# Seven sets of expert weights, down weights on GpSimd's queue, and eight value pages outside the ring

## The reference

```python
h = rmsnorm(x); z = h @ w_in                      # nine parts, 1024 -> 8192
ret = retention_output(retention(q_r, k_r, v_r, state_ret), g)      # 4 heads, decayed states
att = moba_attend(rope(q_a), keys, values)        # 8 sample rows read 8 pages each of cache_k, cache_v
y   = x + (gate_r * (ret @ w_ret_o) + gate_a * (att @ w_att_o)) @ w_o
h2  = rmsnorm(y)
group = top1(h2 @ w_router); two = top2 inside the group (8 experts each, 4 groups)
y  += sum over the two experts of  g_e * (silu(h2 @ w_gate[e]) * (h2 @ w_up[e])) @ w_down[e]
out = rmsnorm(y) * norm_final
```

## Time and profile before

| | us |
|---|---|
| median of 3 runs | 768.91 (768.21 to 770.3) |
| profiled execution | 769.54 |
| its span | 767.7 |
| TensorE busy | 653.7 (85%) |
| VectorE, ScalarE, GpSimd busy | 308.1, 141.3, 139.2 |
| read from HBM, written | 235.00 MB, 9.11 MB |

### The profile page before, as it was taken

How to read it: one execution, slowest core, us unless ns; L and a number is a source line. 1 busy time by engine, 2 the same in 40 slices (tenths; PEclk the granted TensorE clock), 3 DMA queues, 4 the chain that set the end, 5 groups by cost and what they waited for, 6 DMA issues and landing times.

```text
span 767.7 us, 13776 instructions
## 1 busy us (share of the span) xinstructions
PE 653.7 (85%) x5037; PEld 459.7 (60%) x5037; DVE 308.1 (40%) x1554; ACT 141.3 (18%) x404; POOL 139.2 (18%) x209
## 2 busy tenths in 40 slices
PE   6999999999899987989998999827996848767593
PEld 4888887787788765744433877626654525443341
DVE  3005988998867775610000221444324201111114
ACT  3222223223235222210010000121110101000012
POOL 0169954761000223200000000011000000000000
PEclk9999999999999999999999999958998969787898
DMA  9939899789978999579999989457699999999971
GB/s 306 273 110 321 284 305 393 263 280 354 360 252 269 338 322 350 171 276 402 399 410 383 291 330 381 174 225 266 245 392 401 388 387 401 402 403 399 415 283 58
DMA packets 93830, 243.00 MB, mean 317 GB/s; under 512 B 8786, under 2 KB 54482, under 8 KB 85442
## 3 DMA queue, kind: packets, MB, share of 16 engines
q1 hardware_dynamic: 56818, 192.99, 67.1%
q10 hardware_dynamic: 31328, 32.00, 12.8%
q0 software_dynamic: 5616, 17.11, 6.5%
HBM read 235.00 MB, written 9.11 MB: 318 GB/s over the span
## 4 chain that ended last, share of the span: by engine, by line
PE 55%; DMA 26%; DVE 14%; issue 2%; SPq 1%; ACT 1%; POOL 0%; DVEq 0%; ACTq 0%; POOLq 0%
PE zps L885 31%; DVE kall L1367 7%; DMA qb<-in_w_down 6%; DMA hT<-in_w_down 6%; PE zps L1202 4%; PE nps L1179 4%; PE nps L1054 4%; DMA ring_all<-in_w_ret_o 4%; DMA ring_all<-in_w_down 3%; DMA out<-sfin 2%; PE nps L856 2%; DMA kall<-in_cache_k 2%; DMA gain<-v_rows 2%; PE zps L856 1%; PE bps L1217 1%
## 5 line engine op out<-in xcount | busy, mean ns | idle before, releaser
L885 PE MATMUL zps<-hT,ring_all 128*128 128x264 f32 x1152 | 276.3, 394 | 1.6 <-DVE hT L1548 1.0
L885 PEld LDWEIGHTS zps<-hT,ring_all 128*128 128x128 f32 x1152 | 218.3, 194 | 45.6 <-issue 5.6
L1367 DVE CUSTOM_DVE_ANT_0 kall<-kall,qb 128x128 f32<-128x128 f32 x512 | 153.2, 366 | 59.8 <-DMA kall<-in_cache_k 57.1
L596 POOL DMA_INDIRECT zatt<-h_rows,tidx_i x16 | 15.1, 943 | 361.3 <-DVEq L1636 199.8
L1054 PE MATMUL nps<-ring_all,zret 128*64 128x512 f32 x256 | 59.1, 600 | 5.4 <-DMA ring_all<-in_cache_v 4.3
L885 PE MATMUL zps<-headT,ring_all 128*128 128x264 f32 x256 | 58.5, 388 | 4.9 <-DMA ring_all<-in_w_ret_o 3.5
L885 PEld LDWEIGHTS zps<-headT,ring_all 128*128 128x128 f32 x256 | 48.2, 190 | 16.0 <-issue 6.0
L1709 DVE TENSOR_TENSOR qdT<-qdT,nps 128x64 f32<-128x64 f32 x32 | 7.1, 221 | 118.6 <-ACT qdT L801 118.1
L645 ACT ACTIVATE zt<-zps 128x264 f32<-128x264 f32 x56 | 21.8, 390 | 153.6 <-PE zps L885 147.5
L1535 DVE TENSOR_TENSOR hT<-zps,zatt 128x264 f32<-128x264 f32 x8 | 3.5, 433 | 96.4 <-PE zps L885 96.3
L1367 DVE DVE_READ_ACCUMULATOR2_ANT scores<- 128x1 f32 x512 | 40.9, 80 | 0.0
(11 more groups left out here) (360 smaller groups left out, 829.1 us busy)
## 6 DMA issues: line engine op xcount, KB each, us to landing
kall<-in_cache_k SPq DMA_DIRECT2D x64, 512.0 KB, 6.5
ring_all<-in_cache_v SPq DMA_DIRECT2D x64, 512.0 KB, 8.1
ring_all<-in_w_in ACTq DMA_DIRECT2D x26, 1024.0 KB, 8.4
ring_all<-in_w_gate SPq DMA_DIRECT2D x12, 1024.0 KB, 18.8
ring_all<-in_w_up SPq DMA_DIRECT2D x12, 1024.0 KB, 21.8
ring_all<-in_w_down SPq DMA_DIRECT2D x12, 1024.0 KB, 14.5
ring_all<-in_w_in SPq DMA_DIRECT2D x6, 1024.0 KB, 13.5
kall<-in_w_gate SPq DMA_DIRECT2D x5, 1024.0 KB, 22.6
```

The costliest lines, as they stand in the source:

```text
L596: pool.indirect_dma_start(out=rows, out_offset=None, in_=h2_rows, in_offset=bass.IndirectOffsetOnAxis(ap=col, axis=0), bounds_check=T - 1, ...
L885: mm = pe.matmul(zps[m % 2][:, 0:T], w[:, k, P * fb:P * (fb + 1)], rhs[:, k, :], start=(k == 0), stop=(k == KT - 1))
L1367: ins = v.tensor_tensor_reduce(kh, kh, qb[b % 2][:, P * h:P * (h + 1)], 1.0, 0.0, ALU.mult, ALU.add, scores[:, pg, AH * b + h:AH * b + h + 1])
```

## The change

- `SETS` is 7. The seventh gate-and-up place is the first 4096 columns of `zatt`, issued when the router's rows have been stored; the seventh down place is in `cst`. To make room, several small tiles now share `rows_a` and `rows_b`, the transposed rows lie in `gain`, and gathers have one buffer, `rows_b`, so each waits for the transposes of the last. `norm_final` is loaded by SyncE when all gate-and-up products are done.
- `V_SOON`: value units 0 to 3 don't pass through the ring. Units 2 and 3 are issued behind key page 53 into `zdec`, 0 and 1 behind the last key pages into `kall`, and only then the ring goes on with `ret_o` 0 and value unit 4.
- All down weights are issued by GpSimd; SyncE issues only gate and up. The last quad's down weights come in column halves.
- `quad_down` stands one expert later (e % 4 of 1 or 2), and the adding halves and the residual products too.
- At the end, the sample rows' products come before the last prompt products, and ScalarE squares the sample rows instead of VectorE's reduction.

```diff
-ADD_AT = {(q, half): 4 * q + 5 + half + 2 * (q == 0) for q in range(NQUAD - 1) for half in range(2)}
+ADD_AT = {(q, half): 4 * q + 6 + half + 2 * (q == 0) for q in range(NQUAD - 1) for half in range(2)}
-SETS = 6
+SETS = 7
+V_SOON = 4
...
-        order += [("v", k) for k in range(N_V) if min(k // 8, 2) == j]
+        order += [("v", k) for k in range(V_SOON, N_V) if min(k // 8, 2) == j]
...
                     for p in range(NB * NPG):
                         key_page(p)
+                        if p == 53:
+                            sp.wait_ge(f_nT, 1)
+                            sp.wait_ge(out_done, 96)
+                            sp.wait_ge(d_T, 1)
+                            sp.wait_ge(v_out, 16)
+                            for j in (2, 3):
+                                value_pages(j, v_soon[j], v_soon_in[j])
+                    for j in range(2):
+                        sp.wait_ge(page_done, NB * NPG - 2 + 2 * j)
+                        value_pages(j, v_soon[j], v_soon_in[j])
...
-            for e in range(SETS, NE + 2):
-                if e < NE:
-                    sp.wait_ge(e_GU, e + 1 - SETS)
-                    gate_up_in(e % SETS, e)
-                if e >= SETS + 2:
-                    sp.wait_ge(e_D, 2 * ((e - 2 - SETS) // 4 + 1))
-                    down_in((e - 2) % SETS, e - 2)
+            sp.wait_ge(h2_out, 48)
+            gate_up_in(6, 6)
+            for e in range(SETS, NE):
+                sp.wait_ge(e_GU, e + 1 - SETS)
+                gate_up_in(e % SETS, e)
...
+            pairs = 0
+            for e in range(SETS, NE):
+                q = (e - SETS) // 4
+                while pairs < min(2 * q + 5, NPAIR):
+                    gather_for(pairs)
+                    pairs += 1
+                pool.wait_ge(e_D, 2 * (q + 1))
+                if e < NE - 4:
+                    down_in(e % SETS, e)
+                else:
+                    down_half(e, 0, d_in[e % SETS])
+            for p in range(pairs, NPAIR):
                 gather_for(p)
-            for p in range(2, NPAIR):
-                gather_for(p)
+            for e in range(NE - 4, NE):
+                down_half(e, 1, d_last)
```

More of the change, by code:

```diff
@@ L196, in build @@
         fcol = sb("fcol", [P, KT])
-        lgs = sb("lgs", [G + NE, T])
+        rows_a, rows_b = sb("rows_a", [P, DM]), sb("rows_b", [P, DM])
+        lgs = rows_b[0:G + NE, 0:T]
         xs = sb("xs", [P, 3, DM])
@@ L261, in build @@
             down_w[i] = ring[(g + 2) % RING]
-        xgT = [zflat[:, 3 * DM + 512 * i:3 * DM + 512 * (i + 1)] for i in range(2)]
+        xgT = [gain[:, 512 * i:512 * (i + 1)] for i in range(2)]
         acT = [scores_f[:, 256 * i:256 * (i + 1)] for i in range(2)]
@@ L320, in build @@
         slot_in = [sem(f"slot_in{i}") for i in range(RING)]
+        v_soon_in = [sem(f"v_soon_in{i}") for i in range(V_SOON)]
         k_in = [sem(f"k_in{i}") for i in range(KRING)]
@@ L349, in build @@
             "t_x", "t_exp", "t_tabs"))
-        x_in2 = [sem(f"xg_in{i}") for i in range(2)]
+        x_in2 = sem("xg_in")
         e_T, e_Tc, e_GU, e_sg, e_ac, e_H, e_Hc, e_D, e_Dc = map(sem, (
@@ L405, in key_page, with value_pages @@
                              cache_k[0, bass.ds(pid, 1)].rearrange("o s h d -> (o s) (h d)")).then_inc(k_in[p % KRING], 16)
+            def value_pages(j, out, signal):
+                for k in range(2):
+                    pid = sp.value_load(ptab[0:1, 2 * j + k:2 * j + k + 1], min_val=0, max_val=NPOOL - 1)
+                    sp.dma_start(out[:, DM * k:DM * (k + 1)],
+                                 cache_v[0, bass.ds(pid, 1)].rearrange("o s h d -> (o s) (h d)")).then_inc(signal, 16)
             for n, (kind, j) in enumerate(UNITS):
@@ L413, in _ @@
                     slot_free(n)
[L414 to L417, removed]
+                    value_pages(j, ring[n % RING], slot_in[n % RING])
                 else:
@@ L511, in turn @@
                 link(pool.tensor_tensor(x2, x2, tb, ALU.add))
+            for lo, hi in ((0, T), (328, 584), (648, DM)):
+                link(pool.memset(rows_b[0:2 * CAP, lo:hi], 0.0))
             a0, _ = COL["rope"]
@@ L592, in _, with gather @@
+            pool.wait_ge(m_done, 8)
+            down_in(2, 2)
+            pool.wait_ge(z_ready, 2 * (N_IN + 2 * N_O + 1))
+            down_in(0, 0)
+            down_in(6, 6)
+            pool.wait_ge(z_ready, 2 * (N_IN + 3 * N_O))
+            down_in(1, 1)
+            down_in(3, 3)
+            pool.wait_ge(l_T, 1)
+            down_in(4, 4)
+            pool.wait_ge(h2_root, 1)
+            down_in(5, 5)
             pool.wait_ge(h2_out, 48)
             pool.wait_ge(t_idx, 1)
-            def gather(par, rows, col):
+            def gather(rows, col):
@@ L605, in _ @@
-            for p in range(2):
+                if p:
+                    pool.wait_ge(e_T, p)
+                gather(xg, tidx_i[0:2 * CAP, p:p + 1])
+            pairs = 0
[9 more added lines that the diff above has]
+                    down_half(e, 0, d_in[e % SETS])
@@ L764, in _ @@
             load_x()
-            act.dma_start(gain[:, :], norm_final.rearrange("(o d) -> o d", o=1).partition_broadcast(P)
-                          .rearrange("p o d -> p (o d)")).then_inc(fgain, 16)
             for k in range(KT):
@@ L1047, in values @@
             def values(j):
-                n = AT["v", j]
                 b = j // 4
-                pe.wait_ge(slot_in[n % RING], slot_value(n))
+                if j < V_SOON:
+                    pages = v_soon[j]
+                    pe.wait_ge(v_soon_in[j], 32)
+                else:
+                    n = AT["v", j]
+                    pages = ring[n % RING]
+                    pe.wait_ge(slot_in[n % RING], slot_value(n))
                 for k in range(2):
@@ L1252, in quad_down @@
                 last = q == NQUAD - 1 and half == 1
+                if last:
+                    pe.wait_ge(d_last, 64)
                 if y_n[0] and not last:
```

168 lines of the change are left out of this document (81 added, 87 removed).

## The result

| | us |
|---|---|
| changed kernel, median of 4 | 807.84 (805.69 to 812.25) |
| kernel before, beside it, median of 4 | 768.56 (767.49 to 770.3) |
| ratio, 95% interval | 1.0502 (1.0468 to 1.0536) |
| forecast | 776, range 752 to 800, slower 0.63 |
| span of the profiled execution | 804.0 (before 767.7) |

The change makes the kernel 5% slower. The direction was the likelier one of the forecast, the place too; the size was more than five times as much, outside the range.

A forecast was written before the change was run, and what follows sets the result against it. Prediction: TensorE and DMA bound the kernel in turn, with DMA full through nearly the whole expert stage. TensorE's end +7.2 us and tail -1.8 gave +5.4; 774 to 776, named 776, range 752 to 800.

The forecast's parts named there:

- The stall, its place and its cause: Expert stage: TensorE waits some 10 us each at transposes of pairs 5, 7, 9, 11, 13 for gathers behind down weights.
- Equal shares: Expert stage, likeliest case: both queues get equal bytes, cycle 33 us, no byte lost or won; 776 us, chance 0.42.
- R: Expert stage: time from release of four down sets to the next transposes; with equal shares 26 us first, then 22.5.
- The sharing rule: How DMA engines share between GpSimd's and SyncE's queues: equal, one third for GpSimd's, or GpSimd's first; equal was taken.
- the one-third case: Rival, expert stage: GpSimd's queue gets one third of the bytes, first R 33 us, cycle 37; 798 us, chance 0.25.
- Start of the experts: First gather issued together with gate and up of expert 6: 0 us taken, bounds -1 and +5.
- a wait at pairs 0 to 4 above 5 us: Start of the expert stage: a stall longer than 5 us at these pairs would show the prediction wrong.
- Value stage: Value pages outside the ring leave 334 to 424 us: -6 us, bounds -8 and -4, capped by TensorE's 7.8 us of waits.
- Front part: Value pages put among the key pages, ret_o issued later: 0 us taken, bounds -3 and +4.
- Seventh set: Expert stage: one set more in flight, 3.1 MB, makes later bytes 7.8 us earlier, counted only if bytes alone bound the stage.
- the faster case: Rival, expert stage: GpSimd's queue served at once, R near 15 us, bytes alone bound the stage; 755 us, chance 0.28.
- Tail: Kernel's end: VectorE's reduction of the sample rows goes, ScalarE squares them earlier; -1.8 us, bounds -2.5 and 0.

The follow-up runs named there:

- gather_between: Changed kernel with each turn's order: gather of pair 2q+5, two down weights, gather of pair 2q+6, two down weights; 773.87 us, 1.0054 of before.
- before_queue_ahead: Kernel before with down weights on GpSimd's queue, both gathers of a turn ahead of the four down weights; 780.39 us, 1.0124 of before.
- before_queue: Kernel before with only the down weights moved to GpSimd's queue, six sets and two gather buffers kept; 817.89 us, 1.0631 of before.
- after_half_up_rows: Changed kernel with the second 4 KB of each up weight row left unfetched from expert 7 on, all partitions; 791.63 us, 1.0260 of before.
- gate_rows_4k: Changed kernel with each gate and each up weight fetched in two transfers of 4 KB rows; 806.11 us, 1.0465 of before.
- downs_sp: Changed kernel with all down weights back on SyncE's list, gathers alone on GpSimd; 760.81 us (0.9847 of before), second measurement 761.80 us (0.9881).
- gather_first: Changed kernel with the gather of pair 2q+5 ahead of the four down weights, that of 2q+6 still behind; 787.84 us, 1.0198 of before.
- downs_sp_6: Six sets in place of seven, otherwise as downs_sp; 771.67 us, 1.0004 of before.

## Why the prediction was wrong

**The stall, its place and its cause: right.** The text named the transposes of pairs 5, 7, 9, 11 and 13, the gather behind four down weights in one queue, and landings of 20 us and more. Four of five came (landings of 25.9, 24.0, 24.1 and 23.8 us), at 16.6 to 19.4 us where "some 10" were expected. Down-weight waits went, and gather_between, before_queue_ahead and before_queue show the cause by changing the order alone and by adding the queue move alone.

**"Equal shares ... a cycle of 10.4 + 22.5 = 33, the DMA's own 33.0: no byte is lost": the step that failed.** The steady cycle is 40.4 us, and both of its terms were too small. The error is the late release (+7.8), a first R of 29.4 us where 26 were taken (+3.3), and three cycles of 43.3, 40.4 and 40.3 where 33 were taken (+25.1), less the 4.5 us by which the one cycle without a wait was shorter than forecast:

| transposes at expert | forecast | measured | error |
|---|---|---|---|
| release of quad 0 | 546 | 553.8 | +7.8 |
| 8 | 572 | 583.1 | +11.1 |
| 12 | 611.6 | 618.2 | +6.6 |
| 16 | 644.6 | 661.6 | +17.0 |
| 20 | 677.6 | 702.0 | +24.4 |
| 24 | 710.6 | 742.3 | +31.7 |
| end of TensorE | 763.4 | 794.1 | +30.7 |

(794.1 is 792.19 + 1.88.) R was 27.4 and not 22.5. I had given SyncE's queue just as many bytes as GpSimd's, 4.46 MB each; in the 28 us from 674 to 702 the DMA moved 10.4 MB at 373 GB/s, so about 6.0 of SyncE's beside 4.46: the 1.6 MB more are 4 us at 397 GB/s, most of the 4.9 that were missing. What the remaining 1 us is wasn't tried. after_half_up_rows shows that SyncE's bytes count. From transposes to release it was 12.8 and 13.0 in two of these cycles and not 10.4, and TensorE's clock bears on that. The granted clock is 0.75 in 661 to 674 and in 702 to 715, where the 10.4 came from a stretch of before at 0.93 (696.6 to 719.8). Behind the stall of 16.75 us the 64 gate and up products of the first expert take 3.64 us, those of the next, six microseconds later, 1.96:

```profile
663.00 3.64 PE L1218 MATMUL nps<-zdec,gain 128*32 128x128 f32 x64
...
669.10 1.96 PE L1218 MATMUL nps<-zret,gain 128*32 128x128 f32 x64
```

The sharing rule, on which I put the choice between three cases, hardly mattered: gate_rows_4k switched it from a third to half and the time stayed.

**The bytes that "are not lost" are.** With 33 us of DMA in a cycle, 40.4 means about 8 idle. I had seen this for the one-third case ("at each transposes both queues are empty") and priced it at 4; it happens with equal shares too, since what may be fetched is bounded by TensorE's place, and TensorE stands: in gate_rows_4k the DMA share from transposes to release is 0.60 and 0.53 (661 to 673, 700 to 713). The rival of one third, 798, was nearer in size, and its rule of the shares is the one that the rows of the changed kernel show (179 packets beside 185). Its place in the range, at the edge, was the fault of the price; but its first R, 33, was too long, and no rival had the steady cycle right. The queue rule of the Trainium skill that the prediction cites (DMA: Bandwidth & Descriptors, Queues, rings and completion order: queues in turn by packets, one ring in order) agrees with the rows of the changed kernel (179 packets beside 185) and of gate_rows_4k (428 beside 431). I gave a stretch of 2 us, 284 to 286, more weight than the rule.

**Start of the experts: 0 taken, about +7 measured.** The first gather was issued at 508.33, 5.3 us earlier than before's 513.60, but the release came 7.8 us later than forecast. The first gather landed after 5.4 us and not 3.7, beside 2.1 MB of gate and up, and TensorE's clock was low for longer (0.66 in 530 to 545, 0.89 before). The bound was +5, and a wait at pairs 0 to 4 above 5 us, which the text had named as a sign of being wrong, came too (6.8 us at pair 0, though before has 5.1 there). How much of the +7 is the single buffer wasn't tried: with seven sets no place for a second one was found. One trace says little about when the stage begins, besides: with the same work ahead of it the first gather was issued at 507.5 in gather_between, 510.4 in downs_sp and 516.0 in gather_first.

**Value stage: -6 taken.** Waits fell by 2.9 us of 7.8, and the pages alone were worth 0.4%, 3 us. The step took the waits' sum as the gain, but behind the first four units the ring's units still keep the DMA at a share of 0.95 and 355 GB/s from 334 to 424, and TensorE still waits for them. **Front part: 0**, nothing in the runs speaks against it; VectorE has no wait for key pages from 270 to 330 us.

**Seventh set: 7.8 us** in the rival's sum, 9 by downs_sp_6. It stood in the faster case alone and was right there in size; what it is worth in the changed kernel, beside the stalls, wasn't measured. **Tail: -1.8.** From TensorE's end to the span's end there were 11.5 us (756.17 to 767.7), now 9.9: -1.6.

## What to carry to other kernels

A queue is an order. Before transfers are moved to another engine's list, look at what small, urgent transfer is already there, and for whom it stands: here 0.26 MB behind 4.2 MB stopped TensorE for 17 to 19 us at four of the quads, and issuing the same bytes from the engine without an urgent transfer made the same design faster than before.

When an engine stands in a stage that the DMA bounds, ask what the DMA may still fetch while it stands. If the places are freed by the engine that waits, the two begin to take turns, and the sum of both is paid and not the larger; price it as wait plus the idle DMA after it.

## What the runs showed of the hardware

- Packets of the software queue and of SyncE's queue come one for one when both hold work (179 to 185, 428 to 431), so the queue with the larger rows gets the larger part of the bytes.
- With each up weight fetched onto 64 of 128 partitions, in 8 KB rows, beside whole gate and down weights, a stretch of 40 us took a full DMA (share 1.02) at 257 GB/s, where whole weights run at 373 to 397: leaving out half of the partitions made the kernel 4% slower than the changed one (842.63 against 807.84), leaving out half of each row 2% faster (791.63).
